# A hybrid attention and mixture-of-experts block: eight weight slots in order of use, TensorE's experts without a loop, the last expert's half rows scattered on their own

## The chip, the cores and the metric

One core of one Trainium2 chip runs the whole program. The metric is the device time of one execution in microseconds; lower is better. Five engines with their own instruction streams do the work (PE or TensorE, DVE or VectorE, ACT or ScalarE, POOL or GpSimd, SP or SyncE), and they wait for each other on semaphores. In this kernel SP computes nothing: it issues the large transfers between HBM and the on-chip memory, in the order of its program, and where it waits for a semaphore everything behind waits too.

## The reference, cut to what matters

```python
x = x + mixed @ w_out[l]                      # after two attention mixers
x = x + moe(rms_norm(x, norm2_g[l]), ...)     # 512 tokens, top 4 of 32 experts
return rms_norm(x, norm_f_g)

def expert_block(args):                       # one expert, its tokens xb
    hc = xb @ w1[e] + b1[e]                   # 1024 -> 2048
    gt = jnp.minimum(hc[:, :D_FF], SWIGLU_LIMIT)
    up = jnp.clip(hc[:, D_FF:], -SWIGLU_LIMIT, SWIGLU_LIMIT)
    glu = gt * jax.nn.sigmoid(SWIGLU_ALPHA * gt)
    return ((up + 1.0) * glu) @ w2[e] + b2[e] # 1024 -> 1024
```

All is float32. An expert's `w1` is 8 MB and its `w2` is 4 MB, so the 32 experts have 384 MB of weights, each read once. The result of an expert, times its gate, is added to the rows of its tokens.

## The kernel before, in words

The first third of the program (to about 520 us) holds the norms, the projections, both mixers and the product with `w_out`. The change leaves its work as it is and only puts some of its tiles into another buffer. What follows is the mixture of experts. Each expert has room for 96 tokens (3 groups of 32).

**TensorE.** `expert(e)` computes the up product of expert e (`up`: a bias product, L1619, then for each of 8 chunks c of the contraction 12 products of 32 x 512, L1625) and then, through `second`, the down product of the expert before it (`down`: bias products, L1632 and L1635, then for each of 8 chunks 4 products of 512 columns, L1643, the half rows, and 4 of 256 columns, L1647, the quarter rows). Two groups of tokens give half rows, the third gives quarter rows. Experts 0, 1, 2 and 31 are written out; experts 3 to 30 are a loop with two experts in its body. The last expert's down product stands alone behind `expert(31)`.

**The weights.** They come in pairs of slabs, 2 MB each (`load_pair`, L628): four pairs of `w1` and two of `w2` for an expert, 192 in all. The tile `ring` has six places of one pair. Pair u of every expert goes to place u, and may be issued when TensorE has used the same pair of the expert before: SP waits for `w1_used` or `w2_used`. SP's order is `w1` of expert e+1 and then `w2` of expert e. The first four pairs are issued at 440 us, during the product with `w_out`. The next two, `w2` of expert 0, come behind the store of the last rows (`store_x2(3)`), which waits for the gather of expert 0's rows.

**Around the first expert.** SP stores the normed rows to a table in HBM (`store_table`, L633), POOL gathers expert 0's rows from it (L831), TensorE turns them (L1593), and `expert(0)` starts. After expert 0's up product TensorE runs `fill_gates` (L1537, L1540), and before expert 1's it waits until DVE has read expert 0's result from PSUM (`hc_free`).

**After the last expert.** ACT copies the two parts of the result out of PSUM (`take_y`, L1157), POOL adds the half rows (L854) and then the quarter rows (L856) to the rows in HBM by indirect transfers, SP reads all rows back (L695), and the last norm follows. SP loads that norm's gains into `xs` (L674) right after the last weights.

Of the kernel before, what the change touches and what calls it, by code (L numbers as in the profile page):

```python
# [37 lines left out]
PIECE = 2048.0  # L38
HOT_PARTS = ((0, 4), (4, 16), (16, E))
# [104 lines left out]
def hybrid_block(nc, x, positions, norm1_g, w_in, cmp_pos_emb, cmp_w1, cmp_w2, fox_f_bias, w_proj_nsa,  # L144
                 w_proj_fox, w_out, norm2_g, router_w, router_b, expert_w1, expert_b1, expert_w2,
                 expert_b2, norm_f_g, rope_freqs, out):
    with ExitStack() as ctx:
# [53 lines left out]
        qk = sb("qk", [P, 4, S])  # L201
# [19 lines left out]
        pcT = sb("pcT", [P, S])  # L221
# [3 lines left out]
        cmp_one = sb("cmp_one", [P, NT, 2, NCP])  # L225
        rope_cos = sb("rope_cos", [P, S])
        rope_sin = sb("rope_sin", [P, S])
# [175 lines left out]
        hc_g, hc_u = ps[:, 0:NG, 0:256], ps[:, 0:NG, 256:512]  # L403
# [16 lines left out]
        def late_of(e, end):  # L420

            return ps[0:CAP, 5, 3 * e:3 * end].rearrange("p (e v) -> p e v", v=3)
# [3 lines left out]
        def up_slab(c, j):  # L426

            return ring[:, c, :].rearrange("p (n j m) -> p n j m", n=2, j=4)[:, :, j, :]
# [32 lines left out]
        slabs_loaded = [sem("slabs_loaded%d" % b) for b in range(6)]  # L461
# [14 lines left out]
        y_ready = sem("y_ready")  # L476
        y_stored = [sem("y_stored%d" % b) for b in range(2)]
# [25 lines left out]
        def _(sp):  # L503
# [116 lines left out]
            def load_pair(e, u):  # L620

                if u < NK // 2:
                    src = expert_w1[0].rearrange("e (p u c) n -> e p u (c n)", p=P, c=2)
                else:
                    src = expert_w2[0].rearrange("e (p u c) n -> e p u (c n)", p=P, c=4)
                at = u % (NK // 2)
                src = src[bass.ds(e, 1), :, at, :] if not isinstance(e, int) else src[e:e + 1, :, at, :]
                sp.dma_start(ring[:, 2 * u:2 * u + 2, :].rearrange("p c n -> p (c n)"), src.rearrange("e p n -> (e p) n"))\  # L628
                  .then_inc(slabs_loaded[u], 16)
# [10 lines left out]
            load_pair(0, 0)  # L640
# [4 lines left out]
            load_pair(0, 3)  # L645
# [3 lines left out]
            sp.wait_ge(out_full, 2 * NT)  # L649
            store_table(NT - 1)  # L650
            sp.wait_ge(xg_loaded[0], 16)
            store_x2(NT - 1)
            for u in range(NK // 2, 6):
                load_pair(0, u)

            def load_w1(e):
                for u in range(NK // 2):
                    sp.wait_ge(w1_used, NK * (e - 1) + 2 * u + 2)
                    load_pair(e, u)

            def load_w2(e):
                for u in range(2):
                    sp.wait_ge(w2_used, 4 * (e - 1) + 2 * u + 2)
                    load_pair(e, NK // 2 + u)

            load_w1(1)
            with sp.Fori(1, E - 1) as e:
                load_w1(e + 1)
                load_w2(e)
            load_w2(E - 1)  # L670


            sp.wait_ge(x2_stored, 16 * (NT + 1))
# [3 lines left out]
            with sp.Fori(0, MAX_EXTRA) as o:  # L677
                with sp.If(total > o):
                    e = sp.value_load(extra[0:1, bass.ds(o, 1)], min_val=0, max_val=E - 1)
                    sp.wait_ge(w2_used, 4 * E)  # L680
# [21 lines left out]
        def _(pool):  # L702
# [150 lines left out]
            def scattered(b, count):  # L853
                pool.indirect_dma_start(out=x2_half, out_offset=bass.IndirectOffsetOnAxis(ap=now_half[b], axis=0),  # L854
                                        in_=yb[b][:, 0:512], in_offset=None, compute_op=ALU.add).then_inc(y_stored[b], 16)
                pool.indirect_dma_start(out=x2_quarter, out_offset=bass.IndirectOffsetOnAxis(ap=now_quarter[b], axis=0),  # L856
                                        in_=yb[b][:, 512:768], in_offset=None, compute_op=ALU.add).then_inc(y_stored[b], 16)
                pool.wait_ge(y_stored[b], 32 * count)

# [45 lines left out]
            take(now_y_ready, 2 * E)  # L905
            take(y_ready, E)
            scattered(1, E // 2)
# [24 lines left out]
        def _(act):  # L932
# [207 lines left out]
            def take_b_up(e):  # L1140

                act.wait_ge(w1_used, NK * e + 1)
                act.activation(b_up, ps[:, NG, :], ACT.Copy).then_inc(b_up_ready, 1)
# [66 lines left out]
        def _(pe):  # L1210
# [418 lines left out]
            def down(b, loaded, used):  # L1629
# [7 lines left out]
                for c in range(NK):  # L1637
# [12 lines left out]
                    if h:  # L1650
                        used(j, ins)
# [678 lines left out]
```

## Time and profile before

| | us |
|---|---|
| median of 3 runs | 1586.25 |
| lowest, highest | 1584.65, 1587.25 |
| the profiled execution | 1587.47 |
| its span in the trace | 1585.8 |
| PE busy | 1536.8 (97%) |
| DVE, ACT, POOL busy | 511.7, 247.1, 311.4 |

The profiled execution is 1.67 us longer than its span, and 1.22 us above the median of the runs. Times inside the trace count from the start of the span. PE busy holds the waits that fall inside pipelined products only in part, so a stage is better read from the starts of its instructions. The DMA share is the mean busy share of 16 DMA engines; it goes a little above 1.00 where packets of two queues overlap on an engine.

### The profile page before, as it was taken

The numbers are of one execution on the slowest core, as the hardware profiler recorded it, in microseconds if no ns is written. First come the engines' busy times: TensorE is split into PE (matmuls) and PEld (weight loads), VectorE is DVE, ScalarE is ACT, GpSimd is POOL, SyncE is SP. The second block draws the span as 40 slices with busy tenths as digits, with TensorE's granted clock in tenths as the row PEclk, the third lists the DMA queues.
The fourth block names the chain that finished last, engine by engine and source line by source line (L and its number), as shares of the span: only waits on it lengthen the run. The fifth ranks groups of instructions, "written<-read, shape, count | busy, mean of one in ns | idle before, by whom it ended". The sixth has DMA issues, their size and how long they took to land.

```text
span 1585.8 us, 31267 instructions
## 1 busy us (share of the span) xinstructions
PE 1536.8 (97%) x13039; PEld 806.9 (51%) x13040; DVE 511.7 (32%) x941; ACT 247.1 (16%) x509; POOL 311.4 (20%) x449
## 2 busy tenths in 40 slices
PE   7999999999999999999999999999999999999993
PEld 4655555665445533355556656655565344433331
DVE  4104555242435442233224222422242223222322
ACT  4213434233422100001000100010001000100001
POOL 2000002341100202122212221221222122221111
PEclk9999999999999999999999999999999999999996
DMA  8121130521261699999999999999999999999985
GB/s 237 27 67 41 40 80 27 170 79 30 66 263 53 252 393 400 410 415 414 409 411 415 415 408 412 415 414 408 411 415 416 406 413 416 414 409 409 417 338 176
DMA packets 108446, 468.17 MB, mean 295 GB/s; under 512 B 29591, under 2 KB 71615, under 8 KB 83794
## 3 DMA queue, kind: packets, MB, share of 16 engines
q1 hardware_dynamic: 94610, 446.55, 70.0%
q0 software_dynamic: 13792, 21.00, 6.0%
q8 instruction: 31, 0.51, 0.1%
q14 instruction: 13, 0.11, 0.0%
HBM read 452.41 MB, written 19.29 MB: 297 GB/s over the span
## 4 chain that ended last, share of the span: by engine, by line
PE 80%; DMA 15%; DVE 2%; issue 1%; ACT 1%; DVEq 0%; PEld 0%; SPq 0%; POOL 0%; ACTq 0%; PEldq 0%; POOLq 0%
PE ps L1625 34%; DMA ring<-in_expert_w 14%; PE ps L1220 12%; PE ps L1643 11%; PE ps L1367 7%; PE ps L1647 5%; PE ps L1557 4%; PE ps L1352 2%; PE ps L1329 2%; PE ps L1339 1%; ACT mixT L1023 1%; PE ps L1507 0%; PE ps L1619 0%; PE ps L1531 0%; PE ps L1229 0%
## 5 line engine op out<-in xcount | busy, mean ns | idle before, releaser
L1625 PE MATMUL ps<-ring,oT_fox 128*32 128x512 f32 x6144 | 673.3, 594 | 3.1 <-DMA ring<-in_expert_w 3.1
L1625 PEld LDWEIGHTS ps<-ring,oT_fox 128*32 128x32 f32 x6144 | 314.1, 110 | 339.5 <-issue 164.2
L1643 PE MATMUL ps<-ring,hT 128*32 128x512 f32 x2048 | 298.7, 596 | 3.2 <-DMA ring<-in_expert_w 3.2
L2183 DVE TENSOR_TENSOR mixT<-ps,mask 128x768 f32<-128x768 f32 x64 | 61.0, 952 | 679.4 <-PE ps L1625 679.4
L1647 PE MATMUL ps<-ring,hT 128*32 128x256 f32 x2048 | 190.3, 381 | 0.0
L1647 PEld LDWEIGHTS ps<-ring,hT 128*32 128x32 f32 x2048 | 105.9, 110 | 115.1 <-issue 64.1
L1367 PE MATMUL ps<-hT,ring 128*128 128x512 f32 x304 | 137.0, 597 | 0.0
L1147 ACT ACTIVATE mixT<-mixT 128x768 f32<-128x768 f32 x32 | 27.0, 845 | 616.8 <-DVE mixT L2187 578.6
L1643 PEld LDWEIGHTS ps<-ring,hT 128*32 128x32 f32 x2048 | 90.9, 110 | 37.7 <-DMA ring<-in_expert_w 3.6
L843 POOL DMA_INDIRECT oT_nsa<-table,pc x93 | 99.9, 1074 | 47.4 <-POOL pc L838 28.0
L1220 PE MATMUL ps<-hT,ring 128*128 128x512 f32 x208 | 90.4, 594 | 0.2 <-ACT hT L953 0.2
L838 POOL COPY pc<-pc 128x3 int32 (+1 forms) x31 | 5.9, 189 | 429.4 <-DMA x<-hT,v_win 395.6
L1367 PEld LDWEIGHTS ps<-hT,ring 128*128 128x128 f32 x304 | 55.4, 190 | 63.7 <-issue 63.7
L1157 ACT ACTIVATE hT<-ps,v_fox 128x512 f32<-128x512 f32 x64 | 33.7, 577 | 273.8 <-PE ps L1647 273.8
L863 POOL COPY pT<-pT 96x32 bf16 (+1 forms) x64 | 15.4, 242 | 253.4 <-ACT hT L1157 239.5
L1220 PEld LDWEIGHTS ps<-hT,ring 128*128 128x128 f32 x208 | 39.1, 190 | 47.9 <-issue 47.7
L1023 ACT ACTIVATE mixT<-ps,st 128x128 f32<-128x128 f32 (+1 forms) x96 | 49.1, 535 | 78.8 <-DVE st L1856 78.8
L854 POOL DMA_INDIRECT x<-hT,v_win x32 | 52.1, 1629 | 43.0 <-POOL v_win L851 24.5
L1557 PE MATMUL ps<-ring,mixT 128*128 128x512 f32 x128 | 59.0, 601 | 0.0
L2172 DVE STREAM_TRANSPOSE oT_fox<-oT_nsa 128x768 f32<-128x768 f32 x31 | 49.7, 1604 | 13.1 <-DVE mixT L2191 6.6
L856 POOL DMA_INDIRECT x<-hT,v_win x32 | 50.5, 1579 | 9.8 <-issue 9.8
L2179 DVE STREAM_TRANSPOSE hT<-mixT 128x768 f32<-128x768 f32 x32 | 51.3, 1603 | 1.1
(303 smaller groups left out, 1150.2 us busy)
## 6 DMA issues: line engine op xcount, KB each, us to landing
ring<-in_expert_w SPq DMA_DIRECT2D x192, 2048.0 KB
ring<-in_w_in SPq DMA_DIRECT2D x28, 512.0 KB, 4.7
ring<-in_w_out SPq DMA_DIRECT2D x8, 512.0 KB, 8.5
ring<-in_w_in SPq DMA_DIRECT2D x1, 2144.0 KB, 12.5
xs<-in_x SPq DMA_DIRECT2D x4, 512.0 KB, 5.1
ring<-in_w_in SPq DMA_DIRECT2D x8, 256.0 KB, 3.6
ring<-in_w_proj_nsa SPq DMA_DIRECT2D x16, 128.0 KB, 3.0
ring<-in_w_proj_fox SPq DMA_DIRECT2D x8, 256.0 KB, 3.2
```

The costliest lines, as they stand in the source:

```text
L843: pool.indirect_dma_start(out=xg_rows[b][:, 256 * g:256 * g + 256], out_offset=None, in_=table_quarter, in_offset=bass.IndirectOffsetOnAxi ...
L854: pool.indirect_dma_start(out=x2_half, out_offset=bass.IndirectOffsetOnAxis(ap=now_half[b], axis=0), in_=yb[b][:, 0:512], in_offset=None, ...
L856: pool.indirect_dma_start(out=x2_quarter, out_offset=bass.IndirectOffsetOnAxis(ap=now_quarter[b], axis=0), in_=yb[b][:, 512:768], in_offse ...
L1023: last = act.activation(probs[:, h, P_OFF[t]:P_OFF[t] + P * (t + 1)], scores(h, t), ACT.Exp, bias=ngm[:, h, t:t + 1], accum_out=sums[:, h, ...
L1220: last = pe.matmul(dst, lhs(c), rhs(c), start=(c == 0), stop=(c == n - 1))
L1367: ins = pe.matmul(w, w_c(c), hT[:, c, :], start=(c == 0), stop=(c == NK - 1))
L1557: ins = pe.matmul(ps[:, u, :], mixT[:, k, t * P:(t + 1) * P], w_o[k][:, n * 512:(n + 1) * 512], start=(k == 0), stop=(k == NK - 1))
L1625: ins = pe.matmul(wide(ps[TG * j:TG * j + TG, g, :]), xT[b][:, g, c, :], up_slab(c, j), start=(c == 0), stop=(c == NK - 1), tile_position= ...
L1643: pe.matmul(ps[TG * q:TG * q + TG, 4, :], gT[b][:, q // 2, c, :], ring[:, NK + j, at:at + 512], start=False, stop=(c == NK - 1), tile_posi ...
L1647: ins = pe.matmul(ps[TG * q:TG * q + TG, 5, 0:256], gT[b][:, 2, c, :], ring[:, NK + j, at:at + 256], start=False, stop=(c == NK - 1), tile ...
L2179: return dve.transpose(gT[b], act_b.rearrange("p g (m c) -> p g c m", c=NK))
L2183: return dve.tensor_tensor(to, half, b_up[:, 256 * n:256 * n + 256].unsqueeze(1).broadcast_to([P, NG, 256]), ALU.add)
```

## The change

Three things change.

First, the places. `ring` keeps its six, and two more come from `xs` (free after the rows are stored) and from a new tile `x0`, which holds what `qk`, the rope tables, `pcT` and `cmp_one` held before. Pairs go to the eight places in the order in which they are issued, so a pair's place changes from expert to expert (`Order`, `Fill`). SP's order stays `w1` of expert e+1 before `w2` of expert e, except at the ends: a pair of expert 1 is issued before the last table store, and its other three before `w2` of expert 0; the last `w2` goes to the places of expert 29's `w2`, and so waits for the down product of expert 29 (before: of expert 30). The gains of the last norm are loaded after the last product.

Second, TensorE's loop is gone: all 32 experts are written out, since the place of each pair differs. Expert 0 uses three other PSUM banks, so that expert 1 need not wait for DVE; `fill_gates` moves into expert 0's up product, behind chunk 2.

Third, in the last down product the half rows of chunks 4 to 7 are finished first and then the quarter rows of these chunks; ACT and POOL take and scatter the half rows while the quarter rows are computed.

```diff
+        x0 = sb("x0", [P, 4096])
+        def pair_slot(k):
+            if k < 6:
+                return ring[:, 2 * k:2 * k + 2, :].rearrange("p c n -> p (c n)")
+            return xs_f if k == 6 else x0[:, :]
+            def w1(self, u):
+                return Fill(self.i, 6 * self.r - 2 + u if self.r else u)
+            def w2(self, u):
+                return Fill(self.i, 6 * self.r + 8 + u if self.r < E - 1 else 6 * self.r + 4 + u)
+                self.slot, self.landed = at % SLOTS, 48 * i + 16 * (at // SLOTS + 1)
...
             sp.wait_ge(out_full, 2 * NT)
+            load_w1_pair(1, 0, 4)
             store_table(NT - 1)
             sp.wait_ge(xg_loaded[0], 16)
             store_x2(NT - 1)
-            for u in range(NK // 2, 6):
-                load_pair(0, u)
+            load_w1_pair(1, 1, 5)
+            sp.wait_ge(x2_stored, 16 * (NT + 1))
+            load_w1_pair(1, 2, 6)
+            sp.wait_ge(table_full, NT + 3)
+            load_w1_pair(1, 3, 7)
...
-                    sp.wait_ge(w1_used, NK * (e - 1) + 2 * u + 2)
-                    load_pair(e, u)
+            def load_w2(e, order):
+                for u in range(2):
+                    if order.r == E - 1:
+                        sp.wait_ge(w2_used, 4 * (e - 2) + 2 * u + 2)
+                    elif isinstance(e, int) and e == 0:
+                        sp.wait_ge(w1_used, 2 * u + 2)
+                    else:
+                        sp.wait_ge(w1_used, NK * e + 2 * (u + 2) + 2)
+                    load_w2_pair(e, u, order.w2(u).slot)
+            def load_w1(e, order):
+                for u in range(4):
+                    if u >= 2:
+                        sp.wait_ge(w1_used, NK * (e - 1) + 2 * (u - 2) + 2)
+                    elif isinstance(e, int) and e == 2:
+                        sp.wait_ge(w1_used, 2 * (u + 2) + 2)
+                    else:
+                        sp.wait_ge(w2_used, 4 * (e - 3) + 2 * u + 2)
+                    load_w1_pair(e, u, order.w1(u).slot)
+            sp.wait_ge(w2_used, 4 * E)
             sp.dma_start(gf_b, norm_f_g.unsqueeze(0).partition_broadcast(P)).then_inc(pos_loaded, 16)
...
+            take(y_half_ready, 1)
+            scattered_halves(1)
             take(y_ready, E)
-            scattered(1, E // 2)
+            scattered(1, E // 2, False)
...
-            take_y(E - 1, 1, E // 2 - 1)
+            for n, (cols, signal) in enumerate(((slice(0, 512), y_half_ready), (slice(512, 768), y_ready))):
+                act.wait_ge(w2_used, 4 * E - 1 + n)
+                act.activation(yb[1][:, cols], y_ps[:, cols], ACT.Copy, scale=gate_y[:, n, E - 1:E]).then_inc(signal, 1)
...
+            def down_last(b, slots, loaded, used):
+                down_bias(b)
+                for c in range(NK):
+                    j = c // 2
+                    if c % 2 == 0:
+                        loaded(j)
+                    ins = down_halves(b, c, slab(slots[j // 2], j % 2))
+                    if c < NK // 2:
+                        ins = down_quarters(b, c, slab(slots[j // 2], j % 2))
+                        if c % 2:
+                            used(j, ins)
+                used(NK // 2 - 2, ins)
+                for c in range(NK // 2, NK):
+                    ins = down_quarters(b, c, slab(slots[j // 2], j % 2))
+                used(NK // 2 - 1, ins)
...
-                if before:
+                if isinstance(e, int) and e == 1:
+                    pe.wait_ge(b_up_ready, 1)
+                    pe.wait_ge(rows_ready, 1)
+                elif before:
                     pe.wait_ge(hc_free, e)
...
+                    if isinstance(e, int) and e == 0 and c == 2:
+                        fill_gates()
...
-            with pe.Fori(0, (E - 4) // 2) as i:
-                expert(2 * i + 3, 1, True)
-                expert(2 * i + 4, 0, True)
-            expert(E - 1, 1, True)
-            second(E - 1, 1)
+            for e in range(E):
+                expert(e, e % 2, e > 0, Order(0, e))
+            second(E - 1, 1, Order(0, E - 1))
```

On SP, from the last stores to the first weights behind them, before (L633 stores a part of the table, L637 a part of the rows, L628 loads a pair):

```order
L633 DMA table<-hT 128x1024 x2
L637 DMA x<-xs 128x1024
L628 DMA ring<-in_expert_w 128x4096 x6
L667 UNCONDITIONAL_BRANCH
```

And now (L665, L669 and L655 are the same three; L661 loads a pair of `w2`; `x` is `x0` in the rows that load weights):

```order
L665 DMA table<-hT 128x1024
L655 DMA ring<-in_expert_w 128x4096
L665 DMA table<-hT 128x1024
L669 DMA x<-xs 128x1024
L655 DMA ring<-in_expert_w 128x4096
L655 DMA xs<-in_expert_w 128x4096
L655 DMA x<-in_expert_w 128x4096
L661 DMA ring<-in_expert_w 128x4096 x2
```

One pair has moved ahead of the last table store, and three more pairs of expert 1 stand where the two of expert 0's `w2` stood.

On TensorE, expert 0's up product and the start of expert 1's, before:

```order
L1625 MATMUL ps<-ring,oT_fox 32x512 x12
L1606 MATMUL ps<-v_fox,ident 32x32 x12
L1625 MATMUL ps<-ring,oT_fox 32x512 x84
L1537 MATMUL ps<-kT_win,qk 96x96
L1540 MATMUL ps<-v_sel,qk 96x3 x32
L1619 MATMUL ps<-pT 32x512 x4
L1625 MATMUL ps<-ring,oT_fox 32x512 x60
```

And now (L1686 is L1625 of before, L1598 and L1601 are `fill_gates`, L1680 is the bias product):

```order
L1686 MATMUL ps<-ring,oT_fox 32x512 x12
L1667 MATMUL ps<-v_fox,ident 32x32 x12
L1686 MATMUL ps<-ring,oT_fox 32x512 x24
L1598 MATMUL ps<-kT_win,x 96x96
L1601 MATMUL ps<-v_sel,x 96x3 x32
L1686 MATMUL ps<-ring,oT_fox 32x512 x60
L1680 MATMUL ps<-pT 32x512 x4
```

`fill_gates` has moved from behind chunk 7 to behind chunk 2. The number of products is the same.

## Rows read from the trace of the kernel before

**Rows 1.** The page: busy tenths and GB/s in 40 slices of the span.
```profile
PE   7999999999999999999999999999999999999993
DMA  8121130521261699999999999999999999999985
GB/s 237 27 67 41 40 80 27 170 79 30 66 263 53 252 393 400 410 415 414 409 411 415 415 408 412 415 414 408 411 415 416 406 413 416 414 409 409 417 338 176
```
**Rows 2.** Waits of TensorE (PE) in the whole span: us, times, longest.
```profile
PE ps L1643 <- DMA ring<-in_expert_w: 3.2, 1, 3.2
PE ps L1625 <- DMA ring<-in_expert_w: 3.1, 8, 0.6
PE ps L1619 <- issue: 1.7, 1, 1.7
```
**Rows 3.** Chain that ended last, pieces in order of time: start, us, what.
```profile
592.21 20.60 PE ps L1625 x191
...
655.15 20.60 PE ps L1625 x192
...
1190.30 20.62 PE ps L1625 x192
1211.07 26.33 DMA ring<-in_expert_w
1237.44 5.40 PE ps L1625 x48
...
1495.32 5.36 PE ps L1625 x48
...
1511.55 20.60 PE ps L1625 x192
1537.70 10.00 DMA ring<-in_expert_w
1547.74 1.93 PE ps L1643 x8
```
**Rows 4.** Weight loads of TensorE, 1524 to 1530 us: the last pair of expert 31's `w1`.
```profile
1526.50 0.13 PEld L1625 LDWEIGHTS ps<-ring,oT_fox 128*32 128x32 f32 x4 [0.41 <-DMA ring<-in_expert_w]
```
**Rows 5.** Stretches: busy of PE, PEld, DVE, ACT, POOL, then PEclk, DMA share, GB/s.
```profile
520.00:525.00 5.00, 4.52 (x45) 4.14 (x44) 3.01 (x15) 1.94 (x4) 0.55 (x1) 1.00 0.12 49
560.00:565.00 5.00, 5.00 (x36) 1.44 (x32) 2.96 (x7) 0.60 (x1) 0.00 (x0) 0.69 0.99 423
565.00:570.00 5.00, 5.00 (x52) 1.61 (x48) 0.00 (x0) 0.00 (x0) 0.00 (x0) 1.00 0.75 272
595.00:600.00 5.00, 5.00 (x52) 1.65 (x48) 0.00 (x0) 0.44 (x1) 2.79 (x2) 1.00 0.96 337
1535.00:1540.00 5.00, 5.00 (x68) 1.96 (x61) 3.77 (x4) 0.00 (x0) 0.00 (x0) 1.00 0.27 66
1545.00:1550.00 5.00, 2.26 (x16) 0.72 (x20) 0.00 (x0) 0.00 (x0) 2.82 (x2) 0.61 0.99 385
```
**Rows 6.** SP's issues in order of time, 401 to 755 us.
```profile
505.20 18.72 SPq L633 DMA_DIRECT2D table<-hT  x2
531.84 0.32 SPq L637 DMA_DIRECT2D x<-xs  x1
```
**Rows 7.** DMA queues of 540 to 700 us: packets, MB, share of 16 engines.
```profile
q8 instruction: 12, 0.20, 0.5%
```
**Rows 8.** PE in order of time, 505 to 600 and 1541 to 1549 us.
```profile
532.10 1.02 PE L1593 MATMUL ps<-ident,oT_nsa 96*128 96x96 f32 x8
...
558.41 0.40 PE L1619 MATMUL ps<-pT 96*32 96x512 bf16 x4 [1.67 <-issue]
558.63 14.76 PE L1625 MATMUL ps<-ring,oT_fox 128*32 128x512 f32 x120
...
1544.02 0.40 PE L1632 MATMUL ps<-pT 96*32 96x512 bf16 x4 [1.22 <-issue]
```
**Rows 9.** ACT and POOL in order of time, 1540 to 1586 us.
```profile
1542.86 1.05 ACT L1157 ACTIVATE hT<-ps,v_fox 128x512 f32<-128x512 f32 x2 [8.22 <-PE ps L1647]
1560.89 1.05 ACT L1157 ACTIVATE hT<-ps,v_fox 128x512 f32<-128x512 f32 x2 [16.98 <-PE ps L1647]
...
1562.73 1.57 POOL L854 DMA_INDIRECT x<-hT,v_win  x1 [5.74 <-ACT hT L1157]
1564.60 1.55 POOL L856 DMA_INDIRECT x<-hT,v_win  x1 [0.31 <-issue]
```

More of the change, by code:

```diff
@@ L1613, in wide, with up @@
                 return c.rearrange("p (n m) -> p n m", n=2)
-            def up(b, loaded, used):
+            def up(b, slots, loaded, used, hc=HC):
                 for j in range(4):
@@ L1637, in down @@
+            def down(b, slots, loaded, used):
+                down_bias(b)
                 for c in range(NK):
-                    j, h = c // 2, c % 2
-                    if h == 0:
+                    j = c // 2
+                    if c % 2 == 0:
                         loaded(j)
-                    for q in range(4):
-                        at = h * D + (q % 2) * 512
-                        pe.matmul(ps[TG * q:TG * q + TG, 4, :], gT[b][:, q // 2, c, :],
-                                  ring[:, NK + j, at:at + 512], start=False, stop=(c == NK - 1), tile_position=(0, TG * q))
@@ L1645, in down @@
[L1645 to L1653 removed]
+                    down_halves(b, c, slab(slots[j // 2], j % 2))
@@ L1655, in expert @@
+            def expert(e, b, before, order):
+                fills = [order.w1(u) for u in range(4)]
                 pe.wait_ge(xT_ready, e + 2)
-                if before:
+                if isinstance(e, int) and e == 1:
+                    pe.wait_ge(b_up_ready, 1)
+                    pe.wait_ge(rows_ready, 1)
+                elif before:
                     pe.wait_ge(hc_free, e)
@@ L1669, in expert, with loaded, second @@
                     pe.wait_ge(parts_taken, 1)
-                up(b, lambda c: pe.wait_ge(slabs_loaded[c // 2], 16 * e + 16) if c % 2 == 0 else None, used)
+                def loaded(c):
+                    if c % 2 == 0:
+                        pe.wait_ge(slabs_loaded[fills[c // 2].slot], fills[c // 2].landed)
+                up(b, [f.slot for f in fills], loaded, used, HC if before else HC_FIRST)
                 if before:
-                    second(e - 1, 1 - b)
-                else:
-                    fill_gates()
-            def second(e, b):
+                    second(e - 1, 1 - b, Order(order.i, order.r - 1))
+            def second(e, b, order):
+                fills = [order.w2(u) for u in range(2)]
+                def loaded(j):
+                    if j % 2 == 0:
+                        pe.wait_ge(slabs_loaded[fills[j // 2].slot], fills[j // 2].landed)
                 pe.wait_ge(gT_ready, e + 1)
@@ L1683, in second @@
                 pe.wait_ge(pick_down_ready, e + 1)
-                down(b, lambda s: pe.wait_ge(slabs_loaded[(NK + s) // 2], 16 * e + 16) if s % 2 == 0 else None,
-                     lambda s, ins: ins.then_inc(w2_used, 1))
+                (down_last if isinstance(e, int) and e == E - 1 else down)(b, [f.slot for f in fills], loaded, lambda j, ins: ins.then_inc(w2_used, 1))
             pe.wait_ge(count_taken, 1)
```

132 lines of the change are left out of this document (77 added, 55 removed).

## The prediction

> **What bounds the kernel now.** I read the page's slices first, then the waits of TensorE, then the chain in order of time, then narrow stretches at both ends of the expert stage. From about 535 us on the DMA slices stand at 9 and PE's too [rows 1], so shares do not tell which of the two is late. The waits seem to say TensorE: in the whole span it waits 6.3 us for weights [rows 2]. The chain says something else. From 592.21 to 1190.30 us there are 19 experts, 31.48 us each, with TensorE never late. From 1211 us on the pieces are loads of 26 to 27 us, with TensorE's last pair of an expert behind each, and from 1237.44 to 1495.32 us there are 8 experts, 32.24 us each [rows 3]. So a pair of weights takes 32.24 / 6 = 5.37 us, an expert's weights come 0.77 us slower than TensorE uses them, and it lives on a lead until about 1211 us. Both halves of the stage have 406 to 417 GB/s [rows 1]: the loads run at the same speed all the way, and the end is where the last loads put it. A load in the chain takes 26.9 us from issue to landing, five pairs' time, so five wait in the queue and the places are not what holds it back in the middle. More places help only if the queue starts earlier, or where it runs dry.
>
> It starts late: 520 to 525 us has 49 GB/s [rows 5], and the loads behind the first four are issued after 531.84 us [rows 6]. It runs dry at 565 us (272 GB/s), a little at 595 us (337), and at 1535 us (66) [rows 5]: there `w2` of expert 31 may only be issued when the down product of expert 30 has used its place, at 1537.70 us, and it lands at 1547.7 [rows 3].
>
> **The change, part by part.** The terms are for the landing of the last pair of expert 31's `w1`, at 1526.50 us before [rows 4], and then for the path behind it.
>
> Head start: the pair put ahead of the last table store goes out when the last product with `w_out` is done, about 519 us, into an idle queue [rows 5]. Every later pair then stands one place further ahead: -5.37 us.
>
> Gaps: at 565 us the queue lacks (412 - 272) / 412 x 5 = 1.7 us, at 595 us 0.9 us. In the new order every pair there has its place free well before its turn (the first pair of expert 2 may go after chunk 5 of expert 0, about 553 us, and its turn comes at about 564). -2.6 us. One new wait could make a gap: expert 1's last pair waits for `fill_gates`, which ends at about 545 us (534.2 + 1.2 + 3 chunks of 2.58 + 1.9 for the small products), and with it wait the `w2` pairs behind it on SP. Two pairs are then still to be moved until about 547.5 us. I take 0, the other end is 2.
>
> Table store: it is issued 18.7 us behind the one before, at about 523.6 us [rows 6], and now has 2 MB ahead of it, issued at 519 us. These need about 5.4 us and a start, until about 525.5 us. Store, gather and so the transposes at 532.10 [rows 8] come later by 0 (if the queues share) to 5 us (all of the pair); I take 1.2. The row store and all weights behind it wait for the gather: +1.2 us.
>
> Code of TensorE: from 540 to 700 us, 5.1 experts of written-out code, 12 packets of 16 KB of instructions were loaded, 0.5% of 16 engines' time, 12.8 us, or 1.07 us each [rows 7]. That is 2.4 packets an expert. The loop held 2 experts' code for 28, so 26 x 2.4 = 62 packets are added, 66 us of one DMA engine. Spread over 16 they cost 4.1 us; bounds are 2.6 us (1.0 MB at 412 GB/s) and 66 us (all on one engine). TensorE itself did not wait in that stretch, so I cost the fetch on its side at nothing.
> The Trainium skill (Runtime: NRT & Kernel Launch, Instruction fetch mechanics) says that crossing a 16 KB block is mostly hidden, and that a taken branch out of the loaded window forces a stall. By the first the 4.1 us would be nothing and the time 1573; by the second the loop's 13 back edges would cost, and their removal would gain. The trace has 31.48 us an expert inside the loop, and 31.47 from 592.21 to 655.15 where its first expert runs [rows 3]: no gain there, I take none. The same skill (DMA: Bandwidth & Descriptors, Why a DMA increments its semaphore by 16 and not by 1) says that a load is complete only when all its engines have posted, which speaks against this change: the slowest engine counts, not the mean.
>
> Sum for that landing: -5.37 - 2.6 + 1.2 + 4.1 = -2.7, so about 1523.8 us.
>
> Expert 1's wait: the 1.67 us before it [rows 2, 8] goes, and 1.9 us with it. Behind that idle time the granted clock was 0.69, between its two levels [rows 5], and 120 rows of products took 14.76 us [rows 8] where 120/192 of 20.60 is 12.9 [rows 3]. `fill_gates` only moves. This gives TensorE 3.6 us of lead, and the end nothing while the loads are late.
>
> The last products: expert 30's down product ended at about 1542.8 us [rows 9]; it follows the landing, so now 1540.1. Then ACT empties the PSUM bank; the last down product began at 1544.02, 1.22 us later [rows 8], and will again. Before, it took until 1560.89 [rows 9], 16.9 us. An expert's down product is 31.47 - 20.60 - 0.2 = 10.65 us; the other 6.2 us are a wait of 3.2 [rows 2] and a granted clock down to 0.61 [rows 5]. `w2` of expert 31 is now the next two pairs behind expert 30's: it lands at 1523.8 + 4 x 5.37 = 1545.3 us, and its second pair is needed at 1541.3 + 0.6 + 5.1 = 1547.0. The wait goes. The clock cost may stay: 1.22 us idle is near the 1.67 that cost 1.9, so I take 1.5, bounds 0 and 1.9. Last product at 1541.3 + 10.65 + 1.5 = 1553.5 us, 7.4 us earlier. Late next is nothing of DMA: the margin of the last pair is 1.7 us.
>
> Half rows: before, the quarter scatter was issued 3.7 us behind the end of the products (1564.60 - 1560.89) [rows 9]. Now ACT has only the quarter rows left, 0.5 us of its 1.05, and POOL's half scatter (1.57 us [rows 9]) starts about 0.4 us before the products end, so the quarter scatter can go at 1.5 us. -2.2 us. The gains of the last norm, 512 KB, now travel beside these scatters: +0.5, bounds 0 and 2.
>
> Sum: -7.4 - 2.2 + 0.5 = -9.1 us, on the profiled execution 1587.47 to 1578.4. The median of the runs is 1.22 us below it: 1577.1.
>
> **Rivals.** (a) TensorE becomes the bound. If the code costs the loads nothing visible, the landing is at 1519.7, and TensorE alone would need it at about 1518. Its floor: expert 2 starts at 592.21 - 3.6 + 1.2 = 589.8, 29 experts of 31.47 bring expert 31 to 1502.4, and the end is at 1502.4 + 20.6 + 0.2 + 10.65 + 1.2 + 10.65 = 1545.7, 15.2 us earlier; with the tail -16.9, a time of 1569. For it: PE without waits with 12 such packets under way. Against: nothing moves on a full queue for free.
>
> (b) The code eats the gain: the slowest engine gets twice its share, 8.2 us. Then -5, a time of 1581; with the full 5 us at the table store too, 1585: no change.
>
> (c) Slower: the packets fall on few engines. The forecast has about 4 of 62 on each; from 4 + 9.1 / 1.07, about 12 or 13 packets on the slowest engine, the kernel is slower than before, and with all on one it is 62 us slower than forecast, 1639. Against: 12 packets had been loaded by 700 us [rows 7]. The seventh pair behind 532 us, the first of expert 2, should land at about 535 + 7 x 5.37 + 1.7 = 574 us and was needed at 592.2: a lead of 18 us. Used up at 0.77 us an expert by 1211 us, 19.7 experts, it was 15. So 3 us are missing, where one engine with all 12 packets would have lost 12. Three or four engines that share them are not excluded.
>
> (d) The head start is given back: SP stands before expert 1's last pair until `fill_gates` is done, and if that comes 5 us later than I put it, or the pair at 519 us delays the gather by all of its time and the first product with it, the queue runs dry for as long as was won. Then the landing moves by +2.7 only, the last products still gain 4.7 by the earlier `w2`, and the tail 1.7: -3.7, a time of 1582.5.
>
> **How the numbers follow.** Forecast 0.55, (a) 0.15, (b) 0.10, (c) 0.10, (d) 0.10. The likeliest's own range is 1573 to 1581 (code 2.6 to 6, clock 0 to 1.9, store 0 to 3). The range to 1569 takes in (a), to 1585 (b) and (d), and leaves (c) out. A measurement can tell 0.2%, 3.2 us, from no change: faster is below 1583.1. Faster gets 0.55 + 0.15, most of (b), 0.06, and half of (d), 0.05; slower gets (c), 0.10; the rest, 0.09, is no change.
>
> **What the profile after would show.** DMA at 300 GB/s or more from 520 to 525 us, and no dip at 565, 595 or 1535 us. PE idle under 0.3 us before expert 1, and its first transposes at about 533.3. The instruction queue with 62 packets more, about 1.0 MB. TensorE's first waits for weights later than 1211 us, and the landing of expert 31's last `w1` pair at 1523 to 1525. From the end of the last product to the quarter scatter 1.5 us. Wrong would be: a landing after 1526.5 us (the code costs more than the head start gives), waits of TensorE with nothing but code missing, or a period above 32.6 us while it waits for weights.

## The result, and the profile after

| | before | changed |
|---|---|---|
| median, us (6 runs each) | 1585.55 | 1591.32 |
| lowest, highest | 1582.84, 1587.25 | 1589.39, 1592.55 |
| ratio, 95% interval | | 1.0036, 1.0024 to 1.0049 |
| profiled execution, its span | 1587.47, 1585.8 | 1591.5, 1589.8 |

The change makes the kernel 0.36% slower. The forecast was 1577.1 us, faster, with a range up to 1585: it was wrong in sign and in size.

The page of the changed kernel, slices and instruction queue, against [rows 1]:

```profile
PE   7999999999999999999999999999999999999992
DMA  8121131521261799999999999999999999999984
GB/s 236 27 61 46 40 80 27 170 79 30 66 262 53 280 424 407 409 414 413 406 411 413 414 404 413 412 412 405 414 413 412 406 411 414 414 409 407 415 336 144
...
q8 instruction: 99, 1.62, 0.4%
```

At this coarse view nothing has happened: the same tenths and the same 405 to 415 GB/s in the expert stage. Only the queue of instruction fetches (packets, MB, share) stands out: 31 packets before, 99 now.

The narrow stretches of the changed kernel (busy of PE, PEld, DVE, ACT, POOL, then PEclk, DMA share, GB/s), against [rows 5]:

```profile
520.00:525.00 5.00, 4.81 (x39) 4.28 (x38) 2.95 (x12) 2.25 (x4) 0.55 (x1) 1.00 0.75 275
525.00:530.00 5.00, 4.52 (x52) 3.99 (x51) 3.01 (x9) 0.23 (x1) 0.18 (x1) 1.00 0.60 249
530.00:535.00 5.00, 3.64 (x38) 3.45 (x37) 2.37 (x4) 0.00 (x0) 3.12 (x4) 0.90 0.25 73
535.00:540.00 5.00, 5.00 (x41) 2.86 (x43) 2.82 (x11) 0.00 (x0) 0.00 (x0) 0.76 1.02 335
...
1535.00:1540.00 5.00, 5.00 (x60) 1.78 (x56) 1.51 (x3) 0.00 (x0) 0.30 (x2) 1.00 0.74 301
1540.00:1545.00 5.00, 5.00 (x68) 2.00 (x63) 4.74 (x6) 0.84 (x1) 0.00 (x0) 1.00 0.50 213
1545.00:1550.00 5.00, 4.03 (x52) 1.43 (x44) 0.20 (x1) 0.90 (x2) 0.00 (x0) 1.00 0.41 174
```

The pair in front of the table store does fill 520 to 525 us, as forecast (49 GB/s before, 275 now). The dips of [rows 5] at 565 and 595 us are gone too (433 and 408 GB/s). The last three rows are the ones to stop at. The last load of weights is issued at 1517.62 us, so the queue should run at full speed and then be empty. Instead the share of the DMA engines falls to one half and stays there, at half the usual rate. That reads as half of the 16 engines being done while the others still bring the last weights; experiment 6 comes back to it.

The chain of the changed kernel in order of time, against [rows 3], and below it TensorE's weight load that waits for the last pair of expert 31's `w1`, against [rows 4]:

```profile
1137.78 36.98 DMA ring<-in_expert_w
1174.80 5.36 PE ps L1686 x48
1201.52 38.68 DMA ring<-in_expert_w
...
1397.25 39.10 DMA ring<-in_expert_w
1436.40 5.36 PE ps L1686 x48
```
```profile
1532.92 0.26 PEld L1686 LDWEIGHTS ps<-ring,oT_fox 128*32 128x32 f32 x8 [0.60 <-DMA ring<-in_expert_w]
```

The first load that TensorE waits for is issued at 1138 us and ends the wait at 1174.8 us; before, these were 1211 and 1237.4 us. Eight experts from 1174.80 to 1436.40 us take 32.70 us each (before 32.24), and the last pair of `w1` is used at 1532.9 us. The prediction had 1523.8. Two of its own signs of being wrong have come: a landing after 1526.5 us and a period above 32.6 us.

The end of the changed kernel, against [rows 9]: ACT, POOL and SP in order of time.

```profile
1559.48 0.69 ACT L1234 ACTIVATE hT<-ps,v_fox 128x512 f32<-128x512 f32 x1 [9.33 <-PE ps L1705]
1561.15 0.47 ACT L1234 ACTIVATE hT<-ps,v_fox 128x256 f32<-128x256 f32 x1 [0.98 <-PE ps L1713]
```
```profile
1560.95 1.57 POOL L911 DMA_INDIRECT x<-hT,v_win  x1 [3.75 <-ACT hT L1234]
1562.82 1.55 POOL L905 DMA_INDIRECT x<-hT,v_win  x1 [0.31 <-issue]
```
```profile
1561.14 0.33 SPq L724 DMA_DIRECT2D xs<-in_norm_f_g  x1
1572.84 1.76 SPq L744 DMA_DIRECT2D ring<-x  x4
```

The quarter scatter (L905) goes out 1.7 us after the products end; before it was 3.7. But SP issues the reads of the rows (L744) only at 1572.84 us, 10.0 us behind that scatter's issue. Before, it was 1569.05 - 1564.60 = 4.45 us. The chain says what SP does in between:

```profile
1561.14 0.33 SPq L724
1561.52 0.48 SPq L726
1562.04 0.19 SPq L726
...
1572.84 0.34 SPq L744
```

L726 reads how many experts have to be computed a second time, because more than 96 tokens chose them, and L727 and L728 are SP's loop over the 21 that there could be. None is here, so every round only counts, compares and branches, and 21 rounds last from 1562.5 to 1572.7 us, 0.49 us each. In the kernel before this loop stood behind the last loads of weights, and SP ran it while TensorE computed. The change puts the wait for the last down product, for the gains of the last norm, in front of it.

### The profile page after: what moved, and what is told of

It is laid out like the page before. It is cut to its first block, busy times and chain, and to the rows that moved or that the text cites. A ratio compares the mean times of both kernels' runs of the same rounds, so it can differ in the third digit from the quotient of the medians.

```text
span 1589.8 us, 31060 instructions
## 1 busy us (share of the span) xinstructions
PE 1534.5 (97%) x13039; PEld 639.2 (40%) x13040; DVE 510.8 (32%) x941; ACT 247.5 (16%) x509; POOL 321.4 (20%) x449
## 4 chain that ended last, share of the span: by engine, by line
PE 79%; DMA 16%; issue 2%; DVE 1%; ACT 1%; SPq 0%; DVEq 0%; PEld 0%; POOL 0%; PEldq 0%; POOLq 0%; ACTq 0%
PE ps L1686 32%; PE ps L1281 12%; DMA ring<-in_expert_w 12%; PE ps L1705 11%; PE ps L1428 7%; PE ps L1713 6%; PE ps L1618 4%; DMA xs<-in_expert_w 2%; PE ps L1413 2%; PE ps L1390 2%; PE ps L1400 1%; ACT mixT L1079 1%; DMA ring<-x 0%; DMA xs<-in_x 0%; PE ps L1680 0%
## 5 line engine op out<-in xcount | busy, mean ns | idle before, releaser
L1686 PE MATMUL ps<-ring,oT_fox 128*32 128x512 f32 x4704 | 513.0, 592 | 6.0 <-DMA ring<-in_expert_w 6.0
L1686 PEld LDWEIGHTS ps<-ring,oT_fox 128*32 128x32 f32 x4704 | 151.3, 110 | 350.2 <-issue 322.3
L1705 PE MATMUL ps<-ring,hT 128*32 128x512 f32 x1472 | 191.6, 592 | 0.0
L1713 PE MATMUL ps<-ring,hT 128*32 128x256 f32 x1472 | 113.1, 379 | 0.0
L1713 PEld LDWEIGHTS ps<-ring,hT 128*32 128x32 f32 x1472 | 47.7, 110 | 110.2 <-issue 110.2
L1686 PE MATMUL ps<-x,oT_fox 128*32 128x512 f32 x720 | 80.1, 593 | 1.4 <-DMA x<-in_expert_w 1.4
L1686 PE MATMUL ps<-xs,oT_fox 128*32 128x512 f32 x720 | 80.2, 592 | 1.1 <-DMA xs<-in_expert_w 1.1
L1215 ACT ACTIVATE hT<-ps,v_fox 128x512 f32<-128x512 f32 (+1 forms) x62 | 32.6, 577 | 257.6 <-PE ps L1713 257.6
L917 POOL COPY pT<-pT 96x32 bf16 (+1 forms) x64 | 23.1, 362 | 225.1 <-ACT hT L1215 210.2
L1705 PEld LDWEIGHTS ps<-ring,hT 128*32 128x32 f32 x1472 | 47.3, 110 | 30.0 <-DMA ring<-in_expert_w 0.2
L905 POOL DMA_INDIRECT x<-hT,v_win x32 | 50.5, 1579 | 9.8 <-issue 9.8
## 6 DMA issues: line engine op xcount, KB each, us to landing
ring<-in_w_in SPq DMA_DIRECT2D x1, 2144.0 KB, 12.3
```

The lines of the kernel that those rows point to most:

```text
L1215: ins = act.activation(yb[b][:, cols], y_ps[:, cols], ACT.Copy, scale=gate)
L1686: ins = pe.matmul(wide(ps[TG * j:TG * j + TG, hc + g, :]), xT[b][:, g, c, :], up_slab(slots[c // 2], c % 2, j), start=(c == 0), stop=(c == ...
L1705: ins = pe.matmul(ps[TG * q:TG * q + TG, 4, :], gT[b][:, q // 2, c, :], rows[:, at:at + 512], start=False, stop=(c == NK - 1), tile_positi ...
L1713: ins = pe.matmul(ps[TG * q:TG * q + TG, 5, 0:256], gT[b][:, 2, c, :], rows[:, at:at + 256], start=False, stop=(c == NK - 1), tile_positio ...
```

## The experiments

They ran in three groups, each beside the kernel before (medians 1585.22, 1585.15 and 1585.23 us). Experiments 6 and 8, the third group, ran on another chip than the rest; since the medians of before agree, their times are compared with the others' directly. Profiled executions can lie 1 to 2 us from their medians, so prices are taken from medians and only places from traces. Brackets behind a median hold the lowest and highest run, behind a ratio its 95% interval.

**1. The code alone.** The kernel before, with TensorE's loop written out and nothing else.

```diff
-            with pe.Fori(0, (E - 4) // 2) as i:
-                expert(2 * i + 3, 1, True)
-                expert(2 * i + 4, 0, True)
+            for e in range(3, E - 1):
+                expert(e, e % 2, True)
```

> The kernel before, with TensorE's loop over experts 3 to 30 written out and nothing else changed. Theory 1 (the added code packets ride on half of the DMA engines and delay every load): 66 to 68 instruction packets more, a period of about 32.7 us instead of 32.24 while TensorE waits for weights, the DMA share near 0.5 while the last pairs land, and the end 8 to 11 us later, ratio 1.005 to 1.007. Theory 2 (the eight places and their order make the loads slower, the code is free): no change, ratio 0.999 to 1.001. My forecast's price, packets spread over 16 engines: 4 us, ratio 1.0026.

Measured: 1597.54 us (1595.63 to 1598.68), ratio 1.0077 (1.0062 to 1.0092). The code costs 12.3 us, three times the forecast's 4 and more than the 8 to 11 of theory 1. Its queue of fetches, its waits of TensorE, its chain, and its last stretches:

```profile
q8 instruction: 99, 1.62, 0.4%
```
```profile
PE ps L1625 <- DMA ring<-in_expert_w: 11.3, 18, 1.7
...
PE ps L1643 <- DMA ring<-in_expert_w: 2.8, 2, 1.8
...
PE ps L1619 <- issue: 1.7, 1, 1.7
```
```profile
991.04 26.33 DMA ring<-in_expert_w
1017.42 5.40 PE ps L1625 x48
...
1440.87 5.40 PE ps L1625 x48
```
```profile
1535.00:1540.00 5.00, 5.00 (x52) 1.46 (x48) 0.00 (x0) 0.00 (x0) 0.00 (x0) 1.00 0.52 199
1540.00:1545.00 5.00, 5.00 (x64) 1.74 (x56) 1.86 (x3) 0.31 (x1) 0.30 (x2) 1.00 0.41 170
```

TensorE never waits for instructions: the one wait put down to "issue" is the 1.7 us of [rows 2]. It waits for weights, first at 1017 us (for a load issued at 991), and 13 experts take 32.57 us each. So the code is paid by the loads. The half share at the end is here too, without any of the other edits.

**2. Half of the code.** Experts 3 to 16 written out, 17 to 30 in a loop of two.

> As the run before, but only experts 3 to 16 are written out and 17 to 30 stay in the loop. Theory 1: about half of the packets (33) and half of the price, 4 to 6 us, ratio 1.003, with the instruction queue silent in the second half. Theory 2: no change.

Measured: 1591.37 us (1589.22 to 1592.60), ratio 1.0039 (1.0026 to 1.0052), 67 packets. 36 packets more than before cost 6.15 us, 68 packets cost 12.3: 0.17 and 0.18 us a packet. The price goes with the number of packets. Of the 67, 44 fall between 540 and 1070 us, about where the written-out experts run, and 7 in the rest of the stage.

**3. SP's loop first.** The changed kernel, with SP's loop over possible second experts put ahead of the last wait.

```diff
-            sp.wait_ge(w2_used, 4 * E)
-            sp.dma_start(gf_b, ...).then_inc(pos_loaded, 16)
             sp.wait_ge(extra_ready, 1)
             ...
                 with sp.If(total > o):
                     e = sp.value_load(...)
+                    sp.wait_ge(w2_used, 4 * E)
...
+            sp.wait_ge(w2_used, 4 * E)
+            sp.dma_start(gf_b, ...).then_inc(pos_loaded, 16)
```

> The changed kernel, with SP's loop over the possible extra experts (21 rounds that do nothing here) ahead of the wait for the last product and the load of the last norm's gains, where it stood before. Theory: this loop of about 10.8 us stood behind the last product and held back the reading of the rows from about 1567 to 1572.8 us; now the rows are read at about 1567, and the kernel is 5 to 6 us faster than the changed one, ratio to before 0.999 to 1.001. Rival: the read waits for the scatters to land, and they are slow beside the gains' load: no difference, ratio 1.0036.

Measured: 1587.81 us (12 runs, 1585.57 to 1590.04), ratio 1.0014 (1.0004 to 1.0024): 3.5 us less than the changed kernel, where 5 to 6 had been expected. Its chain has the scatter's landing in front of the reads again, where the loop stood:

```profile
1561.93 4.65 DMA x<-hT,v_win
1566.64 0.33 SPq L746
1567.02 6.12 DMA ring<-x
```

**4. Places without code.** A pair's place depends on the expert only in experts 0 to 2 and 31 and is fixed in between, so TensorE's loop of two can stay (experts 5 to 30). The head pair (here the first of `w2` of expert 0), the eight places, the other PSUM banks, the half rows and the edit of experiment 3 are kept.

```diff
-            for e in range(E):
+            for e in range(5):
                 expert(e, e % 2, e > 0)
+            with pe.Fori(0, (E - 6) // 2) as i:
+                expert(2 * i + 5, 1, True)
+                expert(2 * i + 6, 0, True)
+            expert(E - 1, 1, True)
```

> Eight places, early pair, moved gate products, early last w2 and split last product as in the changed kernel, and SP's loop ahead of the last wait; but from expert 3 on each pair has a fixed place, so that TensorE's loop of two experts stays for experts 5 to 30. Theory 1: 5 to 7 instruction packets more than before, TensorE waits little for weights, its last product ends at 1546 to 1550 us and the span is 1571 to 1575, ratio 0.991 to 0.993. Theory 2 (the places themselves slow the loads): span above 1580.

Measured: 1577.45 us (1575.91 to 1580.81), ratio 0.9956 (0.9939 to 0.9973), 36 packets. It beats the kernel before by 7.8 us and the changed one by 13.9. Its waits, its chain and its last stretches of weights:

```profile
PE ps L1700 <- DMA ring<-in_expert_w: 1.5, 4, 0.5
```
```profile
1303.12 26.51 DMA ring<-in_expert_w
...
1329.67 5.40 PE ps L1700 x48
```
```profile
1535.00:1540.00 5.00, 3.78 (x56) 1.55 (x52) 0.00 (x0) 1.05 (x2) 0.00 (x0) 1.00 0.75 321
...
1540.00:1542.00 2.00, 2.00 (x28) 0.73 (x24) 0.00 (x0) 0.00 (x0) 1.57 (x1) 1.00 0.20 82
```

TensorE waits for weights only from 1330 us on (for a load issued at 1303), and no half share stands at the end of the stream. The profiled execution's span, 1574.8 us, is within the expected 1571 to 1575; the ratio is 0.003 to 0.005 above the expected one.

**5. A loop of four.** Experiment 3's kernel, its places repeating every four experts, with TensorE's experts 3 to 30 as a loop whose body is four experts.

```diff
-            for e in range(E):
+            for e in range(3):
                 expert(e, e % 2, e > 0, Order(0, e))
+            with pe.Fori(0, (E - 4) // 4) as i:
+                for r in range(3, 7):
+                    expert(4 * i + r, r % 2, True, Order(i, r))
+            expert(E - 1, 1, True, Order(0, E - 1))
```

> The kernel with SP's loop moved ahead of its last wait (the experiment before last), but TensorE's experts 3 to 30 stand in a loop whose body is four experts instead of being written out; the places in the ring repeat every four experts, so nothing else changes. Theory A (what costs is instruction packets fetched while the weights stream, and a body of four experts no longer fits where one of two experts does): some 95 to 100 packets on the queue of instruction fetches, and the time stays within 0.2% of the written-out kernel's. Theory B (a body of four experts still fits, so it is fetched once): 36 to 46 packets, TensorE waits for weights only from about 1300 us on, and the time lies 8 to 11 us below the written-out kernel, near 1578 us. Theory C (not the fetches but the order of the ring or the fixed places cost the time): as long as the written-out kernel even with under 50 packets.

Measured: 1618.98 us (1618.30 to 1620.63), ratio 1.0216 (1.0202 to 1.0230), 114 packets. None of the three theories has this: more packets than theory A's 95 to 100, and a time 31 us above the written-out kernel. Its waits of TensorE, and PE around the first way back of the loop:

```profile
PE ps L1682 <- issue: 32.5, 6, 5.7
```
```profile
747.49 0.61 PE L1715 MATMUL ps<-x,hT 128*32 128x256 f32 x8
753.82 0.62 PE L1682 MATMUL ps<-pT 96*32 96x512 bf16 x4 [5.71 <-issue]
```

Seven rounds have six ways back, and at each TensorE stands for 5.4 us on average, waiting for nothing but its own instructions. The kernel before, with a body of two experts, has no packet on the instruction queue from 700 to 1500 us. So a body of two is not fetched again, and a body of four is: between 560 and 1600 us it has 98 packets, the changed kernel 84. That the stop is the fetch of the loop's start behind the branch fits this; nothing else was tried for it. The clock pays as well: PEclk in and behind such a stop is below 1:

```profile
750.00:755.00 5.00, 1.18 (x8) 0.46 (x12) 0.00 (x0) 0.00 (x0) 3.22 (x2) 0.67 0.99 413
755.00:760.00 5.00, 5.00 (x36) 1.26 (x32) 0.00 (x0) 0.60 (x1) 0.00 (x0) 0.65 1.01 368
```

The Trainium skill (Runtime: NRT & Kernel Launch, Instruction fetch mechanics) says both things: that straight code is prefetched, its cost mostly hidden, and that a taken branch out of what is loaded stalls. The trace agrees with the second, a stop of 5.4 us. "Hidden" holds for TensorE's instruction stream in experiment 1 and not for the kernel, which paid 12.3 us through its DMA engines.

**6. Experiment 4 with the code.** Experiment 4's kernel, experts 5 to 30 written out; no load, place or wait differs.

> The fastest kernel so far (fixed places from expert 3, SP's loop ahead of its last wait) with one edit: TensorE's experts 5 to 30 are written out instead of standing in its loop. Every load, place and wait stays. Theory A (written-out code costs by its packets, here 99 instead of 36, whatever the order of the ring): 9 to 12 us slower than the kernel with the loop, near 1588 us, TensorE waiting for weights from about 1150 us on, and the DMA engines' share near one half between 1540 and 1545 us. Theory B (the order of the eight slots in the changed kernel costs part of the 10.4 us between the written-out kernel and this one): 3 to 7 us slower than the kernel with the loop.

Measured: 1589.80 us (1589.35 to 1590.86), ratio 1.0031 (1.0019 to 1.0043): 12.35 us above experiment 4, for 63 packets. Theory A, just above its upper end of 12. The price of the code is the same with the old places (12.3) and with these (12.35). The kernel with this code and fixed places is no faster than experiment 3's, with the code and the changed kernel's order (1587.81), so the order of the ring costs nothing. Its stretches of the end have the same half share:

```profile
1540.00:1545.00 5.00, 5.00 (x68) 2.01 (x64) 4.74 (x6) 0.84 (x1) 0.00 (x0) 1.00 0.51 216
1545.00:1550.00 5.00, 4.38 (x60) 1.59 (x52) 0.56 (x1) 0.55 (x1) 0.00 (x0) 1.00 0.43 180
```

The traces hold the start and length of every packet, and from them one can count the 16 KB packets of weights that are under way at one moment: 16 while all engines work. In experiment 4 this number has fallen to half at about 1539.5 us, and the last packet ends at about 1541.5. Here it has fallen to half at 1540.4 us, as early as without the code. But then it stands at 8.0 for 8 us, and the last packet ends at about 1552.7 us, 11 us later than without the code. The changed kernel does the same (half at 1539.5, then 8.0, the end at 1552.3). So the code delays 8 of the 16 engines, by 8 to 11 us, and the other 8 not at all, and 11 of the 12.35 us are the slowest engine's delay.

**7. No head pair.** Experiment 3's kernel, the first pair of expert 1 issued behind the row store instead of ahead of the last table store.

```diff
-            load_w1_pair(1, 0, 4)
             store_table(NT - 1)
             sp.wait_ge(xg_loaded[0], 16)
             store_x2(NT - 1)
+            load_w1_pair(1, 0, 4)
```

> The kernel with SP's loop moved ahead of its last wait, but the first pair of w1 of expert 1 is issued after the store of the last table's last row instead of ahead of that table's store: the queue of weights has nothing to carry while the table is stored and gathered. Theory A (the queue of weights bounds the end, and the head pair is the head start of the change, minus 5.4 us in my sum against plus 1.2 for the later table): the gather lands about 1.2 us earlier than with the pair, expert 1 waits longer for its weights, and the whole is 3 to 5 us slower. Theory B (the head pair's bandwidth was taken from the table and the gather, so that it gives nothing): within 1 us of the kernel with it.

Measured: 1592.23 us (1589.69 to 1592.31), ratio 1.0041 (1.0028 to 1.0053): 4.4 us above experiment 3. Theory A. From issue of the table store to issue of the gather it is 528.84 - 525.19 = 3.65 us here and 528.59 - 523.86 = 4.73 us with the pair, so the pair delays the gather by 1.1 us (in the changed kernel it is 529.82 - 524.95 = 4.87 us). My terms were -5.37 and +1.2.

**8. The same in the kernel with the loop.** Experiment 4's kernel without its head pair.

> The fastest kernel so far, with the first pair of w2 of expert 0 issued after the store of the last table's last row instead of ahead of that table's store. In the written-out kernel the same edit cost 4.4 us. Theory A (the stream of weights still bounds the end of the kernel with the loop, since TensorE is late from 1303 us on): 2.5 to 4.5 us slower than with the pair. Theory B (with the loop TensorE itself bounds the end, so that the head start is slack): within 1 us, or up to 1.2 us faster since the table is stored earlier.

Measured: 1579.39 us (1578.19 to 1581.68), ratio 0.9964 (0.9951 to 0.9977): 1.9 us above experiment 4, between the two theories, and the intervals of the two ratios overlap. With the loop TensorE waits for the loads only in the last fifth of the stage, so a head start may be worth less. That it is worth something is not shown.

**9. A second early pair.** Experiment 4's kernel, with one more pair issued right behind the last table store, ahead of the wait for the gather.

```diff
             store_table(NT - 1)
+            load_w2_pair(0, 1, 5)
             sp.wait_ge(xg_loaded[0], 16)
             store_x2(NT - 1)
-            load_w2_pair(0, 1, 5)
```

> The fastest kernel so far (fixed places from expert 3, TensorE's loop kept, SP's loop ahead of its last wait), with the pair of w2 of expert 0 that is issued after the wait for the last gather issued ahead of that wait, right behind the store of the last table. In the kernel without this edit the DMA engines' share between 525 and 530 us was 0.30 and between 530 and 535 us 0.53. Theory A (this idle time is a hole in the stream of weights that the end of the program pays for): 1 to 3 us faster, the share of these ten microseconds above 0.7. Theory B (the pair's packets stand ahead of the gather's, so that the gather lands later and TensorE starts its experts later): the gather 1 to 4 us later, and no gain or up to 3 us slower.

Measured: 1581.18 us (12 runs, 1579.30 to 1584.46), ratio 0.9978 (0.9969 to 0.9988): 3.7 us slower than experiment 4, though the intervals of the two ratios just touch. The direction is theory B's, the size above its 3. The chain around the gather, in experiment 4 and then here, and the stretches here:

```profile
528.33 1.26 DMA oT_nsa<-table,v_win
```
```profile
528.79 6.41 DMA oT_nsa<-table,v_win
```
```profile
525.00:530.00 5.00, 4.93 (x55) 4.59 (x51) 2.32 (x5) 0.23 (x1) 1.21 (x1) 1.00 1.01 419
530.00:535.00 5.00, 2.33 (x27) 1.84 (x25) 2.36 (x4) 0.00 (x0) 2.09 (x4) 0.83 0.57 225
535.00:540.00 5.00, 4.67 (x28) 2.87 (x32) 2.81 (x11) 0.00 (x0) 0.00 (x0) 0.50 0.49 161
```

The first hole was filled (0.30 in experiment 4, 1.01 here), but the gather's small transfer, issued behind 2 MB, takes 6.41 us instead of 1.26. The row store and its weights, which SP issues behind the gather, come later too, and a new hole opens at 535 us. It is what rival (d) described, one pair further on.

**10. No half rows.** Experiment 3's kernel with the last down product, ACT's copy and the scatters as they were before.

> The kernel with SP's loop moved ahead of its last wait, but the last expert's down products, the take of y and the scatter are whole (768 columns at once, one ScalarE instruction and one GpSimd scatter after all products), as in the kernel before. Theory A (the split takes 2.2 us from the tail, as in my sum): 1.5 to 2.5 us slower. Theory B (the first half's scatter delays the second on GpSimd's queue, or the landing of the scatter is bound by the number of descriptors rather than by bytes): no difference, or faster by up to 1 us.

Measured: 1587.74 us (12 runs, 1584.26 to 1588.60), ratio 1.0012 (1.0004 to 1.0021). With the split it was 1587.81: no difference, where I had summed 2.2 us. Its chain of the end:

```profile
1563.59 5.46 DMA x<-hT,v_win
1569.11 0.33 SPq L746
1569.49 4.64 DMA ring<-x
```

From the end of the products to the reads it is 1569.11 - 1559.88 = 9.2 us here and 1566.64 - 1560.25 = 6.4 us with the split. So the split brings the reads 2.8 us forward. But then SP takes 3.79 us for the issue of the four reads with the split and 1.75 without, and the rows come 6.12 us and 4.64 us later. The two profiled executions end 1.0 us apart, the medians not at all. Why the reads are slower when they come earlier behind the gains' load was not found.

## Why the prediction was wrong, by its own steps

**What bounds the kernel: right.** The loads set the end. The head pair, which gives TensorE no lead, was worth 4.4 us (experiment 7); my two terms for it make -5.37 + 1.2 = -4.2. The gaps of [rows 5] were filled as forecast.

**Code of TensorE: the term that failed.** The number of packets was right (62 forecast, 68 measured), and their time was near (1.07 us forecast; 0.4% of 16 engines over the span is 1.03). The step "spread over 16 they cost 4.1 us" was not: the code costs 12.3 us, in experiments 1 and 6, and by halves in experiment 2. What the runs showed in its place: the code holds up 8 of the 16 engines, and the loads end with the slowest one (experiment 6). That the packets themselves fall on these 8 is the reading that fits; the records name no engine. 68 packets on 8 engines are 68 x 1.07 / 8 = 9.1 us, and the growth of the period, 0.33 us an expert in experiment 1 and 26 experts more of written-out code, gives 8.6. The 8 do not end together but within 4 us, which may hold the rest of the price; why some of the 8 are later stays open. Engines also end some us apart without the code (before, the share in steps of 2 us from 1530 us is 0.67, 0.44, 0.15), but with no level of one half.

My argument against rival (c) was a lead of 18 us against 15 at 1211 us: 3 us missing where 12 packets had been loaded. I used it only to exclude a single engine. The dip at 595 us, 0.9 us by my own count, belongs to these 3, and the other 2.1 make 0.18 us a packet, which is what experiments 1 and 2 measured. It is a rough estimate, a difference of two large numbers. Times 62 it would have been 11 us instead of 4.1, and the forecast 2 us below before, no change.

**What SP does after its last load: a step I didn't take.** I costed the gains' load behind the last product with 0.5 us and named what travels beside it, but not what is queued behind the wait on SP. It is a loop of 21 empty rounds, 0.49 us each: 5.6 us in the trace of the changed kernel (1572.84, where 1562.82 + 4.4 = 1567.2 was due), 3.5 us in the medians of experiment 3.

**Half rows: right at the issue, nothing in time.** 1.7 us from the products to the quarter scatter, 1.5 forecast. In the changed kernel the scatter is not what SP comes out of last, and with the loop moved away the reads give the gain back (experiment 10). The -2.2 us is 0.

**Clock of the last products: 0, not 1.5 us.** The last down product takes 1561.1 - 1550.25 = 10.9 us at a granted clock of 1.00, with 1.22 us of idle time before it. `w2` of expert 31 is there in time: the 3.2 us wait went, though only half of the engines bring its last packets.

**Expert 1's wait: right, but the lead was smaller.** Of TensorE's waits, [rows 2] had 1.7 us at the up bias product; the changed kernel has no such row. This execution begins the stage 1.4 us later for reasons outside of the change (the last product with `w_out` ends at 520.34 us instead of 518.97). From there to expert 2 it is 592.30 - 520.34 = 72.0 us, before 592.21 - 518.97 = 73.2: 1.3 us gained, where 3.6 - 1.2 = 2.4 were forecast. The missing 1.1 us lie ahead of expert 0, which starts 2.2 us later against the last product with `w_out` than before (537.31 - 520.34 = 17.0 us, before 533.79 - 518.97 = 14.8): while the gather is late TensorE stands still, and the granted clock is 0.90 and then 0.76 from 530 to 540 us. The loads set the end, so it cost nothing here.

**The sum again.** Last `w1` pair at 1532.9 instead of 1523.8, 9.1 us: that offset of 1.4 and the code's 8.2 (12.3 - 4.1) make 9.6, half a us too many. Last product at 1561.1 instead of 1553.5, 7.6: the same, less the clock's 1.5. Reads of rows 11.7 us behind it instead of 8.2 - 2.2 + 0.5 = 6.5, 5.2 more. Together 12.8 of the 13.1 us by which the profiled execution missed 1578.4. In medians the miss is 1591.3 - 1577.1 = 14.2 us: code 8.2, SP's loop 3.5, half rows 2.2, clock -1.5, together 12.4, and 1.8 us that no run explains.

The result is rival (c), slower because packets fall on few engines, with SP's loop on top. Its threshold was "about 12 or 13 packets on the slowest engine"; the measured 12.3 us are 11.5 packets of 1.07. I gave it one chance in ten. The code is the larger part: with SP's loop moved away the kernel is still 0.14% slower than before (experiment 3), less than the 0.2% that I called a difference, and with the code out as well it is faster (experiment 4).

## What to carry to other kernels

Where a kernel is bound by loads, ask of written-out code what it adds to the DMA engines and how many of them carry it; a lead that is missing in the trace of before may be that price, so multiply it out. If a loop must stay for that reason, make the places repeat with its body and keep the body small enough: experiment 4 has all that the change wanted, with the loop of two, and is 0.44% faster than before. And when a wait moves, read every instruction behind it on its engine, loops that do nothing among them.

## What the runs showed of the hardware

- Instruction fetches cost the loads more than an even share of the DMA engines: 63 to 68 packets of 16 KB cost a stream of loads 12.3 us where an even spread would have cost 4 to 5. The mean share and GB/s of the stage do not show it (405 to 415 GB/s in both); the end of the stream does, at 0.50 and 213 GB/s: 8 engines end when they do without the code, the other 8 end 8 to 11 us later (experiments 4 and 6).
- A loop of two experts on TensorE (about 5 packets of code, at 2.4 an expert) runs without fetches; one of four (about 10) fetches its code again in each round and stands 5.4 us at each way back.
- 2 MB ahead of a gather of rows delayed its landing by 5.2 us when issued right behind the table store that the gather waits for (6.41 against 1.26), and its issue by 1.1 us when issued 4.6 us ahead of that store.
- A round of an empty loop on SP, with a count, a comparison and a branch, takes 0.49 us (21 rounds in 10.2 us).
- A wait of 1.22 us in front of the last down product cost no clock (1.00 after it); a stop of 5.71 us that ended at 753.8 us left 0.65 from 755 to 760 us.
